# Who copies the high part of the turned SwiGLU rows in the expert blocks

## Time and profile before

| | |
|---|---|
| time, median of 3 runs | 2355.57 us (2350.88 to 2357.18) |
| the profiled execution: span (its page gives no other time for it) | 2351.6 us |
| experts stage in it, from the first turned rows to the last down projection | about 1720 to 2315 us |
| TensorE matmul busy, whole span | 2150.2 us (91%) |
| VectorE busy | 1410.3 us (60%) |
| ScalarE busy | 1025.9 us (44%) |
| GpSimd busy | 845.0 us (36%) |
| mean granted TensorE clock | 0.957 |

### The profile page before, as it was taken

The page is one execution under the profiler, slowest core; times in us unless marked ns, Lnnn a source line. Parts: engine busy times, 40 slices in busy tenths (PEclk is TensorE's granted clock), DMA queues, the critical chain, the costliest instruction groups (busy, mean ns, idle before and its releaser), DMA issues. The chain is left out here.

```text
span 2351.6 us, 26496 instructions
## 1 busy us (share of the span) xinstructions
PE 2150.2 (91%) x10128; PEld 1736.6 (74%) x10128; DVE 1410.3 (60%) x1688; ACT 1025.9 (44%) x1350; POOL 845.0 (36%) x614
## 2 busy tenths in 40 slices
PE   7999999998898995999999789999789999999992
PEld 1278878887787884888888667777667787877882
DVE  1549541100333324888988546345488899998993
ACT  2332311111234445556655334433246576666762
POOL 6300000111456654567766422210123444543531
PEclk9999999999999997999999999999889999999996
DMA  8733415222654765343554675564379955559425
GB/s 312 239 101 90 124 49 192 85 73 68 225 171 153 186 161 198 96 144 120 159 135 122 174 216 179 175 228 148 153 270 368 366 165 161 167 168 352 119 46 169
DMA packets 267113, 401.36 MB, mean 171 GB/s; under 512 B 30630, under 2 KB 190502, under 8 KB 260204
## 3 DMA queue, kind: packets, MB, share of 16 engines
q1 hardware_dynamic: 237004, 242.34, 32.8%
q0 software_dynamic: 27968, 147.89, 20.1%
q10 hardware_dynamic: 2016, 9.45, 1.1%
HBM read 404.32 MB, written 88.67 MB: 210 GB/s over the span
## 5 line engine op out<-in xcount | busy, mean ns | idle before, releaser
L2948 DVE TENSOR_TENSOR ex_w_lo<-ex_raw,ex_w_hi 128x2048 fp32r<-128x2048 f32 x186 | 416.1, 2284 | 39.1 <-ACT ex_w_hi L2810 38.9
L2810 ACT ACTIVATE ex_w_hi<-ex_raw 128x2048 fp32r<-128x2048 f32 x182 | 337.6, 1909 | 173.9 <-DMA ex_raw<-in_w_up_dram,rt_w_rows 84.9
L861 POOL DMA_DIRECT2D vals<-rows_out x40 | 21.8, 545 | 431.3 <-ACT rows_out L853 431.3
L2680 POOL DMA_INDIRECT ex_raw<-in_w_up_dram,rt_w_rows x60 | 79.7, 1329 | 133.3 <-DVE ex_w_lo L2948 127.2
L2680 POOL DMA_INDIRECT ex_raw<-in_w_down_dram,rt_w_rows x30 | 53.2, 1775 | 184.0 <-DVE ex_w_lo L2948 165.2
L2422 PE MATMUL mo_ps<-mo_branch_hi,mo_w_hi 128*128 128x512 f32 x256 | 105.9, 414 | 8.2 <-POOL mo_branch_lo L2213 4.4
L948 PE MATMUL ml_u_ps<-half_hi,ml_u_w_hi 128*128 128x512 f32 x256 | 106.6, 416 | 6.5 <-ACT ml_u_exp L966 6.5
L948 PE MATMUL gl_u_ps<-half_hi,gl_u_w_hi 128*128 128x512 f32 x256 | 107.7, 421 | 3.2 <-ACT gl_u_exp L966 3.2
L853 ACT ACTIVATE rows_out<-rows_ps 128x512 f32<-128x512 f32 x40 | 24.0, 600 | 198.3 <-PE rows_ps L820 198.3
L2739 PE MATMUL ex_g_ps<-ex_w_hi,ex_x_hi 128*128 128x512 f32 x248 | 103.2, 416 | 6.6 <-DVE ex_x_lo L2953 6.6
L2739 PE MATMUL ex_y_ps<-ex_w_hi,ex_hidden_hi 128*128 128x512 f32 x248 | 100.4, 405 | 7.1 <-DVE ex_w_lo L2948 7.1
(11 more groups left out here) (447 smaller groups left out, 6090.8 us busy)
## 6 DMA issues: line engine op xcount, KB each, us to landing
fr_w<-in_w_mod_dram SPq DMA_DIRECT2D x10, 2048.0 KB, 9.9
ml_u_w<-in_w_in_dram SPq DMA_DIRECT2D x32, 512.0 KB, 5.1
gl_u_w<-in_w_in_dram SPq DMA_DIRECT2D x32, 512.0 KB, 5.2
vals<-rows_out POOLq DMA_DIRECT2D x40, 256.0 KB, 2.3
first_values<-vals SPq DMA_DIRECT2D x20, 512.0 KB, 4.5
gl_v<-vals SPq DMA_DIRECT2D x20, 512.0 KB
ml_rows<-scan_rows SPq DMA_DIRECT2D x16, 512.0 KB, 5.7
out_gates<-ml_u_out SPq DMA_DIRECT2D x32, 256.0 KB, 2.5
```

The lines of the kernel that those rows point to most:

```text
L2680: pool.indirect_dma_start(out=raw[:, q, :], out_offset=None, in_=sources[q], in_offset=bass.IndirectOffsetOnAxis(ap=w_rows[:, q, b:b + 1], ...
L2810: act.activation(hi[:, q, h], raw[:, q, h], ACT.Copy).then_inc(hi_done[q], 1)
L2948: dve.tensor_tensor(lo[:, q, at], raw[:, q, at], hi[:, q, at].bitcast(F32), ALU.subtract)\
```

```diff
@@ ScalarE, step(b) @@
                 if more(b):
                     x_hi(b + 1)
                     split_hi(b + 1, 1)
+                act.wait_ge(s["t_h"], b + 1)
+                if late(b, 1):
+                    act.wait_ge(made[2], b)
+                act.activation(ht_hi[:, :], h_ps[:, :], ACT.Copy).then_inc(s["h_hi"], 1)
                 split_hi(b, 2)
@@ VectorE, step(b) @@
                 if more(b):
                     x_lo(b + 1)
                     split_lo(b + 1, 1)
-                dve.wait_ge(s["t_h"], b + 1)
                 if late(b, 1):
                     out(b - 1)
-                dve.tensor_copy(ht_hi[:, :], h_ps[:, :]).then_inc(s["h_hi"], 1)
                 dve.wait_ge(s["h_hi"], b + 1)
                 dve.tensor_tensor(ht_lo[:, :], h_ps[:, :], ht_hi[:, :].bitcast(F32), ALU.subtract)\
                     .then_inc(s["h_lo"], 1)
```

## The result

The change makes the kernel slower: 2361.82 us (median of 7 runs) against 2353.25 us of the kernel before (7 runs beside them), a ratio of 1.0038 with a 95% interval of 1.0025 to 1.0051, or 9 us. The profiled execution has a span of 2359.5 us, 7.9 more than before; its granted clock is 0.957, as before. The text on record said 2350.6, and gave "slower" a chance of 0.04.

The account below looks back on a forecast made before the run. Shared-expert blocks were taken as bound by TensorE, VectorE and late loads together, new-expert blocks by DMA. Gains of 4.3 (short intervals) + 0.6 (start) + 0 + 0.1 (tail) = 5.0 us gave 2350.6 us, range 2345.0 to 2356.5.

Parts of the forecast that it names:

- The six short intervals: Gaps between SwiGLU products set by VectorE alone, 17.45 to 17.46 us: each 0.71 shorter, 4.3 us in all.
- T: Start of a block's SwiGLU product on VectorE; TensorE's next up projection starts at its previous start + 17.75 or T + 1.86, whichever is later.
- its cover: ScalarE's copy and wait for the transposes fit before VectorE needs piece 2: cost 0, with 1 us to spare.
- The start: First copy, ahead of the load of piece 2 and before the DMA engines are full: 0.6 us gained.
- the six DMA-bound ones: Six intervals before 1875, where every block brings a new expert and DMA share is 1.01: gain 0.
- The tail: Last block, nothing covered: VectorE's split of piece 2 waits for ScalarE's copy of its first half; gain 0.1 us.
- Rival A: Faster: DMA-bound blocks follow VectorE (4.3 more), no clock loss (1.65 more), or all 31 copies count (22 us); chance 0.22.
- hang on a landing counted from T: nothing: Eight intervals, 17.6 to 22.9 us, wait for piece 0's late load, whose chain starts from T or earlier: gain 0.
- The nine intervals that I put at nothing: The eight with late piece 0 loads, plus one whose piece 0 is copied just as VectorE comes to it: gain 0.
- the 1.65 that I kept behind the last stall: TensorE's block after its last stall takes 19.40 us, 1.65 over 17.75, put to the granted clock and expected again.
- B: Slower: ScalarE's wait for the transposes delays VectorE's splits and next loads in 14 blocks, 8.1 us, 2363.7; chance 0.05.
- C: Absorbed: ScalarE and VectorE wait on each other, or stalls grow and clock losses recur; gain 0 to 2, 2354.5; chance 0.13.

Follow-up runs that it names:

- e2: The kernel before plus, on ScalarE, the change's two waits and a same-size copy from SBUF into a spare tile, VectorE untouched: 2351.69 us, ratio 1.0008.
- e5: The changed kernel plus a VectorE wait for its own output of the previous block, ahead of the SwiGLU rows' low part, no copy: 2347.61 us, ratio 0.9980.
- e3: The kernel before with VectorE's copy and its wait left out from block 1 on and given to no engine: 2367.64 us, ratio 1.0067.
- e6: The changed kernel plus a spare VectorE copy in the old place, without VectorE's wait for it: 2369.38 us, ratio 1.0062.

## Why the prediction was wrong

**Right:** VectorE's own block (16.75 forecast, 16.73 measured). The six short intervals of the 15 between T = 1875.43 and the stall: 4.3 less, as summed. The price of ScalarE's copy (577 and 594 ns), and its cover: e2 shows it costs nothing that can be told. The start: the first interval is 0.73 shorter, but the six DMA-bound ones behind it are 1.6 longer, so that the 0.6 that was put did not reach T = 1875.43. The tail: the down projection starts 7.44 us after the one ahead of it has ended (2306.93 to 2314.37), 7.48 before; 0.1 less was put, and from the last product to the down projection it is 12.83 us, 12.93 before. Rival A has nothing for it: the six DMA-bound intervals did not shrink in sum. The tail of the kernel after, VectorE and TensorE:

```profile
2306.93 1.28 DVE L2964 SCALAR_TENSOR_TENSOR ex_y<-ex_y_ps,rt_row_weight,ex_gate 128x1024 f32<-128x1024 f32 x1 [4.70 <-PE ex_y_ps L2741]
...
2314.37 0.80 PE L2739 MATMUL ex_y_ps<-ex_w_hi,ex_hidden_hi 128*128 128x512 f32 x1 [7.01 <-DVE ex_w_lo L2952]
```

**The step that failed** is "hang on a landing counted from T: nothing", said of eight intervals, with the sentence that it rests on, "No DMA moves: GpSimd's and SP's orders are as before". The order was as before; the duration of the issues was not. The load of piece 0 went out at T + 3.14, and I took that for a constant of the kernel. It is the end of a queue of issues on GpSimd whose lengths depend on what VectorE runs beside them, and it became T + 8.0 in the seven blocks in which the load of piece 2 and the scatter-add behind it missed their handovers. The nine intervals that I put at nothing, the one at the limit among them, are 10.0 us longer in the same 15 (5.7 more in all, where 4.3 less was put); the one that was bound by nothing but VectorE, with piece 0 ready "just as VectorE comes to it", is the example above, 17.45 to 20.06. Further on there are two new stalls of TensorE, at 2218.21 and 2272.47, where I had none. And the 1.65 that I kept behind the last stall became 2.4: the block takes 20.13 us (2161.89 to 2182.03) instead of 19.40. The granted clock was 0.88 in 2162 to 2182, and 0.91 in 2157 to 2177 before, so the term was the clock's, as put, but lower than the 0.97 that I had read from a longer window.

The rows could have warned. The issue of the earlier trace rows takes 1.78 us and that of the earlier trace rows 2.28, and the same instruction takes 0.99 us where no split runs beside it. I read those lengths, and did not ask what they were waiting for. The first ends 1.0 us after VectorE goes from one half of a split to the next: the engines shared something, and the change took an instruction and a wait out of exactly that sequence.

**The size, had the mechanism stayed away:** e5 is the change with the issues left as they were: 2347.61 against 2352.38, 4.8 us less. The sum said 5.0. So the sum was near for VectorE's time, and wrong about what else the old copy's wait did. The terms agree less than the total: in e5's profile the six short intervals give 3.6 us, the nine that were put at nothing 1.7, and the first one 0.7, while the six DMA-bound ones cost 1.0.

**The rivals.** B's 2363.7 lies 1.9 from the result, but that is chance: e2 has B's mechanism and no loss, e3 the loss and no mechanism of B's. A right number from a wrong cause is no forecast. C's growing stalls are what one sees, but with the opposite cause: they grow since loads are late, not since TensorE is early.

**What supports the cause, and what stays open.** The Trainium skill, "SBUF — State Buffer", section "Who interferes with whom", says that a VectorE instruction with two inputs in SBUF contends with a GpSimd instruction that reads SBUF. The traces agree: the indirect issues, which read row numbers from SBUF, are held beside the split (two SBUF inputs), and freed 0.9 to 1.6 us after VectorE goes to an instruction with an input in PSUM. The same section says that a tensor_tensor was not seen to stall DMA issue; for these indirect DMAs the runs differ, 4.48 us instead of 0.99. That it hangs on a wait of VectorE for its own result is shown by six kernels with one in GpSimd's old order (248 handovers, none missed) and three without (81 got in, 51 missed). With GpSimd's new order the same holds: two kernels with a wait (115 handovers, none missed), one without (60 got in, 8 missed). Why 81 still got in without it, the traces say in part: in after, e3 and e6 all 72 handovers that stand at most eight starts behind a pause of VectorE, whatever it waited for, let the issue in, and all 51 missed ones are among the 60 that stand eleven or more behind it. So it may be the pause that counts, and the wait for its own result only what makes one in every block; that reading comes from the traces alone. How it works inside the engine isn't shown. One reading is that without a pause VectorE's queue runs ahead and the next instruction stands ready at the port when the last one leaves; nothing here measures that, and it would not say why 9 of the 60 got in. Nor have I taken apart the 1.6 us of the DMA-bound intervals, or why e3 and e6 lose more than the change, 18 and 17 us against 9. e3's ten executions spread from 2350.36 to 2372.05 us, and its trace, with its 16 held issues, is of one of 2361.03: it shows a loss like the change's and not the median's.

## What to carry to other kernels

Read the *length* of GpSimd's DMA issues, not only their order: an indirect issue that takes more than its shortest form is being held by VectorE, and its end is no constant. Before taking an instruction and its wait off VectorE, ask which queue had lived on the gap that the wait made; a wait for its own result once a block cost 0.1 us each time here and was worth about 14 in all. And order GpSimd's issues so that as few as possible stand between the split that frees a buffer and the load that is on the chain (the gather and the scatter-add went ahead of piece 2, and piece 0 went out 0.9 us after T instead of 3.1); that alone was worth 0.7%.

## What the runs showed of the hardware

An indirect DMA's issue on GpSimd takes 0.96 us (gather) or 0.99 (load) by itself, but is held while VectorE subtracts with both inputs in SBUF: 2.28 us if it gets in at the next handover, 4.48 if it misses one, 9.35 at worst (a gather), for four such instructions in a row. A semaphore wait of VectorE for its own result, at any of the three places tried in the block, left no handover missed; VectorE's copy without such a wait left 19 issues held. In the three kernels without a wait and in GpSimd's old order, no issue missed a handover that stood at most eight VectorE starts behind a pause (72 of 72), and 51 of 60 missed one that stood eleven or more behind it. Taking a 0.68 us copy off VectorE, with no work put in its place, made the kernel 17.9 us slower.
